# Opening of a two-block transformer kernel: low halves of three weight tiles move from GpSimd to VectorE, and the start of ScalarE, VectorE, TensorE and the load queue is reordered

## The reference

```
kv = rms_norm(mem, mem_gain) @ w_kv            # mem is 256 x 1024
km = rms_norm(kv[..., :MEM_WIDTH]...)          # keys: normed per head, times k_gain
vm = kv[..., MEM_WIDTH:]...                    # values
h = rms_norm(x, norm_gain[l]); cols = h @ w_in_a[j]
qm = rms_norm(q_mem ..., q_gain)               # queries: columns of cols
s = qm km^T * ATTN_SCALE; p = softmax(s); o = p vm
```

## Time and profile before

| | us |
|---|---|
| median of 3 runs | 1880.17 (1879.79 to 1880.75) |
| the profiled execution | 1879.63 |
| its span | 1877.8 |
| TensorE busy | 1840.6 (98%) |
| VectorE busy | 1147.7 (61%) |
| ScalarE busy | 938.7 (50%) |
| GpSimd busy | 588.5 (31%) |

### The profile page before, as it was taken

How to read it: one execution, slowest core, us unless ns; L and a number is a source line. 1 busy time by engine, 2 the same in 40 slices (tenths; PEclk the granted TensorE clock), 3 DMA queues, 4 the chain that set the end, 5 groups by cost and what they waited for, 6 DMA issues and landing times.

```text
span 1877.8 us, 25493 instructions
## 1 busy us (share of the span) xinstructions
PE 1840.6 (98%) x10128; PEld 1588.0 (85%) x10128; DVE 1147.7 (61%) x2028; ACT 938.7 (50%) x1107; POOL 588.5 (31%) x131
## 2 busy tenths in 40 slices
PE   8899999999998999999999999999999999999998
PEld 7688888888897988888888888899888889888887
DVE  7788878776888787222776322567522287862227
ACT  7455555455653554444554544453444455544443
POOL 2000000000000003888100888400588800058880
PEclk9899999999999999999999999999999999999999
DMA  9344444454243335655543555544655543365551
GB/s 360 112 159 156 143 164 152 180 196 155 93 166 131 120 128 195 215 191 192 187 181 136 181 194 189 188 190 165 227 199 192 190 177 135 112 233 199 193 190 65
DMA packets 53049, 325.56 MB, mean 173 GB/s; under 512 B 8624, under 2 KB 11056, under 8 KB 15568
## 3 DMA queue, kind: packets, MB, share of 16 engines
q1 hardware_dynamic: 45328, 310.49, 45.2%
q10 hardware_dynamic: 7616, 13.59, 2.1%
HBM read 323.02 MB, written 1.05 MB: 173 GB/s over the span
## 4 chain that ended last, share of the span: by engine, by line
PE 85%; DVE 10%; issue 2%; ACT 2%; DMA 1%; DVEq 0%; ACTq 0%
PE project L1102 31%; PE output L1102 31%; PE turn L1500 5%; PE project L1500 5%; PE project L1506 2%; PE turn L1506 2%; PE turn L1323 2%; DVE wlo L1962 2%; PE output L1288 1%; PE output L1263 1%; DVE arena L2302 1%; DMA raw<-in_units 1%; DVE arena L2079 1%; DVE arena L2325 1%; PE turn L1242 1%
## 5 line engine op out<-in xcount | busy, mean ns | idle before, releaser
L1059 POOL TENSOR_TENSOR wlo<-raw,whi 128x2048 fp32r<-128x2048 f32 x127 | 588.3, 4664 | 1240.8 <-ACT whi L1569 1224.1
L1569 ACT ACTIVATE whi<-raw 128x2048 fp32r<-128x2048 f32 x289 | 547.0, 1910 | 342.6 <-PE project L1500 166.2
L1102 PE MATMUL project<-whi,XT 128*128 128x512 f32 x1376 | 453.3, 400 | 11.4 <-ACT arena L1578 9.0
L1962 DVE TENSOR_TENSOR wlo<-raw,whi 128x2048 fp32r<-128x2048 f32 x162 | 368.3, 2285 | 23.1 <-ACT whi L1569 20.0
L1102 PEld LDWEIGHTS project<-whi,XT 128*128 128x128 f32 x1376 | 259.7, 189 | 67.0 <-ACT arena L1578 8.2
L1102 PE MATMUL output<-whi,YTh 128*128 128x512 f32 x736 | 288.1, 392 | 1.5 <-DVE YTl L2456 1.5
L1102 PE MATMUL output<-whi,YTl 128*128 128x512 f32 x736 | 287.1, 390 | 0.0
L1102 PE MATMUL output<-wlo,YTh 128*128 128x512 f32 x736 | 286.9, 390 | 0.0
L2740 DVE TENSOR_TENSOR arena<-project,arena 128x256 f32<-128x256 f32 x48 | 20.4, 425 | 409.1 <-ACT arena L1918 409.1
L1102 PE MATMUL project<-wlo,XT 128*128 128x512 f32 x688 | 268.9, 391 | 0.0
L1102 PE MATMUL project<-XT,whi 128*128 128x256 f32 x1184 | 219.0, 285 | 0.1
(11 more groups left out here) (283 smaller groups left out, 2386.8 us busy)
## 6 DMA issues: line engine op xcount, KB each, us to landing
raw<-in_units SPq DMA_DIRECT2D x290, 1024.0 KB, 4.8
arena<-in_ln_g ACTq DMA_DIRECT2D x8, 512.0 KB, 5.4
arena<-in_ln_b ACTq DMA_DIRECT2D x8, 512.0 KB, 7.3
raw<-in_units SPq DMA_DIRECT2D x2, 512.0 KB, 7.3
tok<-in_mem SPq DMA_DIRECT2D x1, 1024.0 KB, 14.4
arena<-in_x_t SPq DMA_DIRECT2D x1, 1024.0 KB, 18.2
xres<-in_x SPq DMA_DIRECT2D x1, 1024.0 KB, 20.1
arena<-in_mem_t ACTq DMA_DIRECT2D x1, 1024.0 KB, 4.5
```

The costliest lines, as they stand in the source:

```text
L1059: pool.tensor_tensor(wlo[:, slot, :], raw[:, slot, :], whi[:, slot, :], ALU.subtract).then_inc(lo_pool, 1)
L1102: mm = pe.matmul(out, x if x_stationary else w, w if x_stationary else x, start=start and i == 0, stop=stop and i == 2, skip_group_check=True)
L1569: act.activation(whi[:, slot, :], raw[:, slot, :], ACT.Copy).then_inc(hi_done, 1)
L1962: dve.tensor_tensor(wlo[:, slot, :], raw[:, slot, :], whi[:, slot, :], ALU.subtract).then_inc(lo_dve, 1)
```

## The change

- `POOL_FIRST` is gone. VectorE makes lo(6), lo(7) and lo(8). The two places where the count of GpSimd's low halves matters for waits are adjusted.
- The opening's order on ScalarE is now: split x, hi(4), hi(5), the keys' bank 0 out, squares of x's rows, the keys' bank 1 out, hi(6), scale_v, hi(7), the queries' bank 0 out, hi(8), the queries' bank 1 out, and then both squares of the queries. Before, the squares of x's rows came ahead of hi(4), and each bank's square came right behind its copy.
- VectorE's order is now: split x, lo(4), lo(5), scales of x, lo(6), keys' norm, lo(7), queries' norm, lo(8), lo(9). `scale_v` has moved to ScalarE, and `init` stands behind unit 7 instead of ahead of unit 6.
- The rows of x are loaded behind unit 5 and ahead of the gain rows, instead of ahead of unit 4.
- In units 0 and 1, TensorE does the two high-by-high products of a slice as soon as the high halves are there, and then waits for the low halves.

```diff
-POOL_FIRST = (6, 7, 8)
@@
+            if squares_last:
+                add("squares_of", **fields)
@@
     split("x", range(8))
-    add("squares", what="x")
-    add("scales", what="x")
     high(4)
     low(4)
+    high(5)
+    low(5)
+    fields = scalar_post(between=[lambda: add("squares", what="x")])
+    add("scales", what="x")
+    high(6)
+    low(6)
     add("scale_v")
-    fields = scalar_post(between=[lambda: high(5)])
-    low(5)
+    high(7)
     add("gains")
     vector_post(fields)
-    for m in (6, 7, 8):
-        high(m)
+    low(7)
@@
-    fields = scalar_post()
+    fields = scalar_post(between=[lambda: high(8)], squares_last=True)
     vector_post(fields)
-    add("init")
@@
             if hq == g == 0:
+                add("init")
                 add("sines", on="sv")
@@
-        on_pool = [m in POOL_FIRST or u[0] == "mlp1" or u[0] == "mlp2" and u[2:] != (1, FF_CHUNKS - 1) for m, u in enumerate(units)]
+        on_pool = [u[0] == "mlp1" or u[0] == "mlp2" and u[2:] != (1, FF_CHUNKS - 1) for u in units]
@@
                     load(raw_xT[:, :, :], a["x_t"], xT_in)
+                elif n == 6:
                     load(xres[:, :, :], a["x"].rearrange("(h p) d -> p h d", p=P), x_in)
-                elif n == 6:
                     load_gains()
@@
-            for m in POOL_FIRST:
-                lo(m, m % RING)
@@
+                    pe.wait_ge(split_hi, 4 * u + k + 1)
...
+                    for b in range(2):
+                        mm = pe.matmul(PP[b][:, :], xh[b], slice_of(whi, n, k), start=u == 0 and k == 0, stop=False, skip_group_check=True)
...
                     pe.wait_ge(split_lo, 4 * u + k + 1)
...
                     for b in range(2):
-                        mm = passes(PP[b][:, :], XH[:, 4 * u + k, b * P:(b + 1) * P], XL[:, 4 * u + k, b * P:(b + 1) * P],
-                                    slice_of(whi, n, k), slice_of(wlo, n, k), u == 0 and k == 0, u == 1 and k == 3)
+                        pe.matmul(PP[b][:, :], xl[b], slice_of(whi, n, k), start=False, stop=False, skip_group_check=True)
+                        mm = pe.matmul(PP[b][:, :], xh[b], slice_of(wlo, n, k), start=False, stop=u == 1 and k == 3, skip_group_check=True)
@@
+                elif kind == "scale_v":
+                    act.wait_ge(scales_ready, 1)
+                    for b in range(2):
+                        act.wait_ge(p_evac[b], 1)
+                        act.activation(vA[0][:, b, :], vA[0][:, b, :], ACT.Copy, scale=scale_of["mem"][b]).then_inc(v_scaled, 1)
```

More of the change, by code:

```diff
@@ L154, in one, with scalar_post @@
                 add("proj", n=len(units) - 1, ahead=False, banks=(1,), begin=False, **f)
-        def scalar_post(on=None, scale_later=False, between=None):
+        def scalar_post(on=None, scale_later=False, between=None, squares_last=False):
             scaled = None if scale_later else "mem" if src == "M" or w[0] == "w_mem_kv" else "x" if w[0] == "w_in_a" else None
-            fields = dict(g=g, tag=tag, src_n=n["src"], heads=len(heads), quad=n["quad"], qk=n["qk"], scaled=scaled, **f)
+            fields = dict(g=g, tag=tag, src_n=n["src"], heads=len(heads), quad=n["quad"], qk=n["qk"], scaled=scaled,
+                          squares_last=squares_last, **f)
             n["qk"] += tag == "qk"
@@ L1113, in sliced_unit @@
                 for k in range(4):
+                    xh, xl = ([x[:, 4 * u + k, b * P:(b + 1) * P] for b in range(2)] for x in (XH, XL))
+                    pe.wait_ge(split_hi, 4 * u + k + 1)
+                    if k < 3:
+                        pe.wait_ge(slice_hi, 3 * n + k + 1)
+                    else:
+                        pe.wait_ge(hi_done, n + 1)
+                    for b in range(2):
+                        mm = pe.matmul(PP[b][:, :], xh[b], slice_of(whi, n, k), start=u == 0 and k == 0, stop=False, skip_group_check=True)
+                        if begin[0]:
+                            mm.then_inc(unit_begun, 1)
+                            begin[0] = False
                     pe.wait_ge(split_lo, 4 * u + k + 1)
@@ L1484, in _ @@
                     n0, g0, q0, i0 = f["n"], f["g"], f["q"], 2 * (FF_CHUNKS - 1) * f["i"]
-                    less = n0 - (4 * FF_CHUNKS - 1) * f["i"] - 1 - len(POOL_FIRST)
+                    less = n0 - (4 * FF_CHUNKS - 1) * f["i"] - 1
                     def mlp1(n, slot, g):
@@ L1590, in load_gla, with square_of @@
                     load(small, a["c_small"], pos_in)
+            def square_of(f, b, buf, sq):
+                if b == 0 and f["qk"]:
+                    act.wait_ge(qk_ready, f["qk"])
+                act.wait_ge(p_evac[b], f["g"] + 1)
+                act.activation(sq[:, b, :], buf[:, b, :], ACT.Square).then_inc(sq_ready, 1)
+                last.other(sq_ready, nth("sq"))
             def post(f):
@@ L1611, in post @@
                         copy_bank(b, g, buf[:, b, :], row)
[L1612 to L1616, removed]
+                        if not f["squares_last"]:
+                            square_of(f, b, buf, sq)
                     elif tag == "gate":
@@ L1734, in _ @@
                         split_high(f, k)
+                elif kind == "squares_of":
+                    for b in range(2):
+                        square_of(f, b, qA, sqA)
+                elif kind == "scale_v":
+                    act.wait_ge(scales_ready, 1)
+                    for b in range(2):
+                        act.wait_ge(p_evac[b], 1)
+                        act.activation(vA[0][:, b, :], vA[0][:, b, :], ACT.Copy, scale=scale_of["mem"][b]).then_inc(v_scaled, 1)
                 elif kind == "sines":
@@ L2413, in _ @@
                         split_low(f, k, f["at"] + x + 1)
[L2414 to L2417, removed]
                 elif kind == "scales":
```

## The result

| | before | after |
|---|---|---|
| median | 1880.46 us of 4 runs, 1879.79 to 1887.49 | 1869.43 us of 4 runs, 1868.97 to 1870.37 |
| profiled execution | 1879.63 | 1869.37 |
| its span | 1877.8 | 1867.6 |
| VectorE busy | 1147.7 | 1140.3 |
| ScalarE busy | 938.7 | 939.6 |

The ratio is 0.9938, with a 95% interval of 0.9925 to 0.9950. The forecast was 1869.6. VectorE took over 3 x 2.3 us of work, gave 0.9 us away (`scale_v`) and is busy 7 us less, since the 13 us that its three small instructions stood were counted as busy.

What follows compares the result with a forecast made beforehand. GpSimd's low halves were taken to hold VectorE's keys' norm, leaving TensorE standing. First transposes at 53.1 instead of 63.67 gave 10.6 us (7.7 standing, 2.8 clock): 1880.17 - 10.6 = 1869.6, range 1866.9 to 1873.4.

Steps and rivals of the forecast that it cites:

- The cause: Keys' norm on VectorE: GpSimd's low halves hold three small instructions, 3 x (4.48 - 0.17) = 12.9 us.
- (d): Rival, VectorE: GpSimd does not hold the small instructions; first transposes at 66.0, total 1882.5; chance 0.02.
- (e): Rival, loads: x's rows land at 43.3 or later and the change loses; chance 0.02, landings from 39.5 0.03 more.
- (a): Rival: longer chain to first transposes, unit 6 landing at 38.0; they start at 55.0, total 1871.5 or 1873.5; chance 0.15.
- (b): Rival: VectorE quicker, TensorE's own floor of 50.6 sets the first transposes; gain 13.1, total 1867.1; chance 0.10.
- T: Landmark on TensorE, the first transposes of a head; forecast at 53.1 instead of 63.67, released by the queries' norm.
- The loads: Load queue in the opening: 2.5 us off units 4 and 5, x's rows behind unit 5, unit 6 at 36.0.
- My 0.6 us on unit 6: Load queue: unit 6 taken at 36.0 instead of 35.4, in case the hold of the last gain's issue ends later.
- Early products count 0: TensorE, units 0 and 1: early high-by-high products save 0.45 us, at most 0.1 arrives, swallowed by unit 4's start.
- (c): Rival: TensorE's clock falls at the first transposes, 1870.6 to 1872.4; later thin places may shift 1.7 either way; chance 0.10.
- cost 0, bound 2: Behind the first transposes: moving init delays VectorE and ScalarE 1.5 to 2 us, hidden; at most 2 us lost.
- the cover: Behind the first transposes: TensorE asks for the second head's exponentials 18.7 us after them; they are ready at about 15.

Runs made afterwards that it cites:

- e1: Kernel before with only the swap: VectorE makes lo(6), lo(7), lo(8), other order as before; 1869.12 us of 4 runs, ratio 0.9933 to before.
- e2: Changed kernel with the three low halves back on GpSimd, new order kept; 1879.61 us of 10 runs, ratio 0.9997 to before.
- e7: Changed kernel plus eight unneeded GpSimd subtractions of two 128x512 tiles, begun when hi(7) is done; 1876.94 us in one run.
- e4: Changed kernel with the three products of a slice in units 0 and 1 together again, behind the low halves; 1869.91 us in one run.
- e3: Changed kernel with the rows of x loaded ahead of unit 4 again; 1871.67 us in one run.
- e5: Changed kernel with the rotary tables' angles (init) ahead of unit 6 again, so ahead of lo(8) on VectorE; 1870.85 us.
- e6: Changed kernel with the queries' squares right behind their copies again; 1878.09 us in one run.
- e9: Changed kernel with gain rows loaded behind unit 6 and the keys' norm ahead of lo(6) on VectorE; 1867.82 us of 5 runs, ratio 0.9934 to before.
- e8: Changed kernel plus eight GpSimd fills of a 128x512 tile with zero, which write and read nothing; 1872.27 us in one run.

## Why the prediction was right, point by point

- The cause. The three long instructions took GpSimd's time and not their own: e1 removes them alone and gains 10.9 us, where the whole change gains 11.0; e2 puts them back and loses all; e7 brings such a hold back with work that nobody needs, and fills do not. This is shown. Of the rivals (d) and (e), the slower ones, nothing was seen. Nor of (a), since unit 6 landed at 35.4 and not at 38.0, nor of (b), since VectorE and not TensorE set T.
- The loads. Forecast: unit 4 26.2, unit 5 28.9, x's rows 31.4 to 33.0, unit 6 36.0. Measured: unit 4 before 25.7, unit 5 28.6, x's rows 31.3 (issued at 16.98, 14.3 to landing), unit 6 35.4. The hold of the queue was there (4.50 us), and ended at 26.7 as before. My 0.6 us on unit 6 for it were wrong, and account for most of the 0.6 us by which T came early.
- ScalarE. hi(4) was not held by its load at all, and hi(5) ended 0.3 us early. scale_v, taken at 1.2 us from the square of the same shape, took 1.32, with 1.22 to the next instruction.
- VectorE. Each norm took 5.3 us, each low half 2.2. T at 53.1 forecast, 52.49 measured.
- TensorE. Unit 4 at 31.5 forecast, 31.18 measured. The wait that the change adds before its bank 1: 0.7 forecast, 0.25 measured. The wait before T: 1.8 forecast, 1.4 measured. "Early products count 0" holds for T (e4).
- Clock. 7.7 us of stand and 2.8 of clock were both regained; the waits of 0.25 and 1.4 us left the clock at 2.4 GHz, so rival (c) did not come about at T. Its second half did: the thin places took back 0.9 us. And in e3 a stand of 2.48 us did bring the clock down, so (c) was a fair rival.
- Behind T. No wait for the second head. The step "cost 0, bound 2" held; e5 shows what the other order costs, 0.3 us. The delay that the cover was to hide was sized too long: 1.5 to 2 us forecast, 0.3 measured. hi(11) begins at T + 8.6 instead of T + 8.3, and the second head's exponentials at T + 13.0 in both kernels. `init` is thirteen instructions and 2.7 us, not fourteen and 2.8.
- The sum. The prediction divides T's gain into 7.7 us of stand and 2.8 of clock, and leaves out others that nearly cancel: measured, unit 4 begins 1.9 us earlier and a wait of 0.5 us at 44.7 goes, while the new waits take 1.7. All together that makes the 11.2 us at T. For the whole: 10.6 us forecast, 10.26 in the profiled execution and 11.0 between medians. The terms that were off, 0.6 us more at T and 0.9 less at the thin places, nearly cancel. The second part of that is luck.

What the prediction did not ask is what the parts are worth apart. The answer is uneven. The swap of engines alone gives T at 53.11. In that kernel TensorE, not VectorE, is the bound, and all the reordering, on ScalarE, VectorE, TensorE and the load queue, adds 0.6 us at T.

## What to carry to other kernels

Here an instruction of VectorE that was 25 times longer than its twin, and ended with an instruction of GpSimd, was a wait and not work. It is counted as busy, so look for it in the longest against the median of one form, not in the busy share. A low half given to GpSimd to unload VectorE cost VectorE twice what it saved: up to 4.5 us of hold for 2.2 us of work, because VectorE's next instructions had two inputs. Where no such instruction meets GpSimd's it costs nothing, as at 1325 in the kernel after, until a small delay moves the two together, as in e6. After such a swap, take the reordering apart before keeping it, and compare by a landmark such as T where totals scatter more than the parts are worth.

## What the runs showed of the chip beyond that

- VectorE and GpSimd take turns: with GpSimd's long subtractions back to back, one two-input instruction of VectorE got in after each, however short it was (0.17 us of work in 4.4 to 4.7 us). With the short ones of e7 it was one of the products or two of the small ones. GpSimd's three subtractions of the opening kept their 4.5 to 4.6 us. Where a VectorE instruction of 0.75 us had begun before it, in e6, GpSimd's took 4.91 instead of 4.62, so GpSimd can be held too.
- At thin places far behind an edit the clock falls differently from kernel to kernel. The same work there ran between 3.4 us (e9) and 17 us (e8, at 503 to 510, 558 to 565 and 582 to 585) at 1.2 GHz. Here is e8, a stretch that was at 2.4 GHz in the kernel after:

```profile
557.80:564.80 7.00, 7.00 (x25) 6.03 (x24) 6.97 (x8) 2.86 (x2) 0.00 (x0) 0.51 0.00 0
```

  e8's T was 0.46 us later than the changed kernel's, its end 2.9 us. Runs of one kernel differ in the same way: e9's at a mean clock of 0.999 took 1867.45, at 0.995 1871.01. So whether the edit or the single execution decides is not shown.
